# Four 64x64 tiles for the transitions of a delta-rule scan, and a recurrence split over two blocks

## The reference, cut to what matters

```python
def step(s, inp):
    r_t, w_t, k_t, v_t, kk_t, a_t = inp
    sa = jnp.einsum('bhvk,bhk->bhv', s, -kk_t)
    s = (s * w_t[:, :, None, :] + sa[..., None] * (kk_t * a_t)[:, :, None, :]
         + v_t[..., None] * k_t[:, :, None, :])
    return s, jnp.einsum('bhvk,bhk->bhv', s, r_t)
```

## Time and profile before

| what | us |
|---|---|
| median of three runs | 2008.89 |
| the profiled execution | 2013.03 |
| its span, first to last instruction | 2011.1 |
| transitions, first matmul to the last copy | 245.8 |
| one turn of the transitions | 29.3 |
| scan, to the first work of the attention | 35.6 |

### The profile page before, as it was taken

One profiled execution on the slowest core, in us unless ns is written; L12 is line 12 of the kernel. 1 busy time (PEld: TensorE's weight loads), 2 busy tenths in 40 slices (PEclk: granted clock), 3 DMA queues, 4 the chain that ended last, 5 costly groups with the idle time before them and its releaser, 6 DMA issues.

```text
span 2011.1 us, 45987 instructions
## 1 busy us (share of the span) xinstructions
PE 1839.5 (91%) x19492; PEld 1740.4 (87%) x19492; DVE 1058.7 (53%) x1790; ACT 812.6 (40%) x1442; POOL 280.9 (14%) x288
## 2 busy tenths in 40 slices
PE   5999999689999688884898999999999999999996
PEld 4988888589999467762898999999999999999995
DVE  4355554334554566657255776652247766432654
ACT  4233322122332266664244564542345555422442
POOL 0012121129990200001000000000000000000000
PEclk8999999899999698886898999999999999999997
DMA  4333434360002686644242343224335322333342
GB/s 152 101 124 121 147 110 141 130 198 4 4 4 49 167 232 185 197 129 173 95 157 72 129 132 133 88 86 137 123 109 173 133 85 94 104 111 106 122 149 87
DMA packets 100570, 241.03 MB, mean 120 GB/s; under 512 B 14290, under 2 KB 18770, under 8 KB 100082
## 3 DMA queue, kind: packets, MB, share of 16 engines
q1 hardware_dynamic: 99794, 235.96, 36.5%
q10 hardware_dynamic: 576, 2.16, 0.3%
HBM read 189.87 MB, written 48.21 MB: 118 GB/s over the span
## 4 chain that ended last, share of the span: by engine, by line
PE 48%; DVE 2%; ACT 1%; issue 1%; POOL 0%; ACTq 0%; DVEq 0%
PE tl_acc L2123 46%; PE tl_ple L2123 1%; PE tl_wide L2088 1%; PE tl_wide L2097 1%; ACT tl_wh L2272 0%; DVE tl_tmp L2396 0%; ACT tl_sq_e L2135 0%; DVE tl_gated L2458 0%; DVE tl_gated L2461 0%; DVE tl_Y L2378 0%; DVE tl_Y L2369 0%; ACT tl_Hh L2241 0%; DVE tl_acc_e L2302 0%; ACT tl_Y L2221 0%; ACT tl_sq_x L2135 0%
## 5 line engine op out<-in xcount | busy, mean ns | idle before, releaser
L2123 PE MATMUL tl_acc<-tl_Hh,tl_wh 128*128 128x264 f32 x1536 | 438.4, 285 | 7.4 <-DVE tl_Hl L2400 7.4
L2123 PE MATMUL tl_acc<-tl_Hh,tl_wl 128*128 128x264 f32 x1536 | 438.0, 285 | 0.0
L2123 PE MATMUL tl_acc<-tl_Hl,tl_wh 128*128 128x264 f32 x1536 | 435.9, 284 | 0.0
L2442 DVE TENSOR_TENSOR tl_wl<-tl_raw,tl_wh 128x1024 fp32r<-128x1024 f32 (+2 forms) x182 | 206.1, 1132 | 419.2 <-ACT tl_wh L2272 419.0
L2272 ACT ACTIVATE tl_wh<-tl_raw 128x1024 fp32r<-128x1024 f32 (+2 forms) x182 | 178.9, 983 | 493.9 <-PE tl_acc L2123 453.9
L2123 PEld LDWEIGHTS tl_acc<-tl_Hh,tl_wh 128*128 128x128 f32 x1536 | 290.0, 189 | 8.7 <-DVE tl_Hl L2400 8.3
L2123 PEld LDWEIGHTS tl_acc<-tl_Hl,tl_wh 128*128 128x128 f32 x1536 | 290.2, 189 | 0.0
L2123 PEld LDWEIGHTS tl_acc<-tl_Hh,tl_wl 128*128 128x128 f32 x1536 | 289.9, 189 | 0.0
L2123 PE MATMUL tl_acc<-tl_Gl,tl_wh 128*128 128x264 f32 x704 | 200.3, 285 | 0.0
L2123 PE MATMUL tl_acc<-tl_Gh,tl_wl 128*128 128x264 f32 x704 | 200.3, 284 | 0.0
L2123 PE MATMUL tl_acc<-tl_Gh,tl_wh 128*128 128x264 f32 x704 | 200.1, 284 | 0.0
(11 more groups left out here) (368 smaller groups left out, 4390.8 us busy)
## 6 DMA issues: line engine op xcount, KB each, us to landing
tl_raw<-dram_w_up SPq DMA_DIRECT2D x88, 512.0 KB, 3.5
as_kT<-dram_k_pool SPq DMA_DIRECT2D x64, 256.0 KB, 3.3
as_vp<-dram_v_pool SPq DMA_DIRECT2D x64, 256.0 KB, 3.2
tl_raw<-dram_w_down SPq DMA_DIRECT2D x32, 448.0 KB, 3.4
dram_projT<-fr_cur SPq DMA_DIRECT2D x26, 528.0 KB, 2.9
fr_raw<-dram_w_in SPq DMA_DIRECT2D x52, 256.0 KB, 3.6
tl_raw<-dram_w_pg SPq DMA_DIRECT2D x32, 320.0 KB, 3.2
ap_dup<-dram_projT SPq DMA_DIRECT2D x16, 512.0 KB, 8.4
```

The source lines that it names most:

```text
L2123: last = nc.tensor.matmul(out[:, n, 0:HP], w[:, u % 2, k, :], z, start=(begin and q == 0), stop=(end and q == 2))
L2442: tt(wl[:, u % 2, 0:kt], raw[:, u % 3, 0:kt], wh[:, u % 2, 0:kt].bitcast(F32), ALU.subtract).then_inc(S["residued"], 1)
```

## The change

1. A head of the pairs 2 and 3 now writes the other half of the partitions (`away`). Four heads (`quads`) stand on four different 64x64 tiles of the array, two of them on the diagonal and two off it. From level to level rows and outputs swap between `home` and `away`. PSUM is regrouped into `even` and `odd`, with pairs 0, 1 and pairs 2, 3 in different banks.
2. `zs` no longer has the identity added by VectorE. The transposed `zs` and the products of level 0 are instead summed in PSUM with a product with `eye`. `tx` and `ux` are two products of 64x64 in place of one of 64x128. The factor 0.5 moves from `ws` to `tn` and `xs`.
3. VectorE masks `m2`, `m4` of a chunk right behind `zs` and waits for `vn_kept` of ScalarE first.
4. SyncE loads the samples' operands right behind the first two chunks, then four chunks, then ten. The constants (four now) are loaded from ScalarE's queue.
5. GpSimd does three of the four steps of the sample recurrence here and the fourth in the scan block. The store of the samples' results moves to the scan block too, behind the last state, and the read of `ysd` behind it. The low parts move to VectorE (`low`, at chunks 6, 8, 10, 12).

```diff
-        heads = [(p, half(h)) for p in range(NPAIR) for h in range(2)]
+        heads = [(p, h) for n in range(2) for p in (n, n + 2) for h in range(2)]
+        quads = (heads[:4], heads[4:])
+        home = lambda p, h: half(h)
+        away = lambda p, h: half(1 - h if p >= 2 else h)
...
-            samples.load(sp, a["wkv"], o["sd"], vec_in, state_in)
-            sp.wait_ge(recurred, NT * RECUR_STEPS)
-            samples.store(sp, o, y_out, state_out)
...
-            samples.recur(pool, recurred)
+            samples.recur(pool, recurred, 0, NT - 1)
...
+            def product(q, cols, w, z, rows, cells, quad=heads, start=True, stop=True):
+                for p, h in quad:
+                    r = rows(p, h)
+                    last = nc.tensor.matmul(q[cells(p, h), p // 2, p % 2, cols], w(r, p), z(r, p), start=start, stop=stop)
+                return last
...
+                for lev in range(NLEV):
+                    rows, cells = (away, home) if lev % 2 == 0 else (home, away)
...
+                        if lev == 0:
+                            for quad in quads:
+                                product(q1[b], left, z, u, rows, cells, quad, stop=False)
+                                product(q1[b], left, one, u, rows, cells, quad, start=False)
...
-                    dve.wait_ge(S["adi0"], c + 1)
-                    tt(zs[:, b], zs[:, b], pairs(eye[:]), ALU.add).then_inc(S["adi"], 1)
...
+                    dve.wait_ge(S["vn_kept"], i * 2 + b + 1)
+                    tt(four(m2[:, b]), q1[b][..., left], pairs(below[:]), ALU.mult).then_inc(S["m2"], 1)
...
             sp.wait_ge(S["state"], NCH)
             sp.dma_start(state_out, states[:, NCH]).then_inc(S["state_out"], 16)
+            sp.wait_ge(S["recurred"], RECUR_STEPS)
+            samples.store(sp, o, S["y_out"], S["sample_out"])
+            sp.dma_start(yt[:], o["ysd"].rearrange("t h a v -> t (h a v)")).then_inc(S["sample_in"], 16)
...
-            for c in range(2):
-                pool.wait_ge(S["high"], c + 1)
-                nc.gpsimd.tensor_tensor(qs[DH:P, 0, c], dup[DH:P, 0, c], qs[DH:P, 0, c].bitcast(F32), ALU.subtract)\
...
+            samples.recur(pool, S["recurred"], NT - 1, NT)
...
+                if c in LOW_AT:
+                    low(LOW_AT.index(c))
```

More of the change, by code:

```diff
@@ L1251, in rwkv_transitions @@
     nc = kit.nc
-    names = ("const_in", "adi0", "adi", "m3", "p1", "p2", "m2", "m4", "turned", "bk_kept", "vn_kept", "zturn", "ut", "made",
-             "zk", "a2v", "a2v_kept", "w", "tx", "tn_kept", "xs", "pr", "phi_kept", "r_kept", "zy", "z_kept", "y_kept")
+    names = ("const_in", "m1", "m3", "p1", "p2", "m2", "m4", "bk_kept", "vn_kept", "zturn", "ut", "made", "zk", "a2v", "a2v_kept",
+             "w", "tx", "ux", "tn_kept", "xs", "pr", "phi_kept", "r_kept", "zy", "z_kept", "y_kept")
     S = {n: kit.sem("rt_" + n) for n in names}
-    first_in, rest_in = kit.sem("rt_first_in"), kit.sem("rt_rest_in")
-    vec_in, state_in, halved, recurred, y_out, state_out = (
-        kit.sem("rt_" + n) for n in ("vec_in", "state_in", "halved", "recurred", "y_out", "state_out"))
+    first_in, next_in, rest_in = (kit.sem(f"rt_{n}_in") for n in ("first", "next", "rest"))
+    vec_in, state_in, halved, recurred = (kit.sem("rt_" + n) for n in ("vec_in", "state_in", "halved", "recurred"))
     with ExitStack() as ctx:
@@ L1307, in turn @@
             def turn(i, first):
                 here = [ds((i * 2 + b) * C, C) for b in range(2)]
+                one = lambda r, p: eye[r, :]
                 for b in range(2):
                     c = i * 2 + b
[L1311 to L1317, removed]
+                    now = here[b]
+                    nr = lambda r, p: NR[r, p, :, now]
+                    if not first:
+                        pe.wait_ge(S["phi_kept"], c - 1)
+                        pe.wait_ge(S["r_kept"], c - 1)
+                    product(q0[b], whole, lambda r, p: BK[r, 0, p, now], nr, home, away)
+                    product(q2[b], left, lambda r, p: BK[r, 0, p, now], one, home, away)
+                    product(q2[b], right, lambda r, p: BK[r, 1, p, now], one, home, away).then_inc(S["p1"], 1)
+                    if not first:
+                        pe.wait_ge(S["z_kept"], c - 1)
+                        pe.wait_ge(S["y_kept"], c - 1)
+                    product(q1[b], whole, lambda r, p: BK[r, 1, p, now], nr, home, away)
+                    product(q3[b], left, lambda r, p: V[r, p, now], one, home, away)
+                    product(q3[b], right, lambda r, p: NR[r, p, 0, now], one, home, away).then_inc(S["p2"], 1)
@@ L1318, in turn @@
                 for b in range(2):
                     c = i * 2 + b
[L1320 to L1328, removed]
@@ L1329, in turn @@
-                    last.then_inc(S["turned"], 1)
+                    z = lambda r, p: zs[r, b, p, :]
+                    pe.wait_ge(S["m1"], c + 1)
+                    pe.wait_ge(S["m4"], c + 1)
+                    for quad in quads:
+                        product(q1[b], left, z, one, away, away, quad, stop=False)
+                        last = product(q1[b], left, one, one, away, away, quad, start=False)
+                    last.then_inc(S["zturn"], 1)
+                for lev in range(NLEV):
+                    rows, cells = (away, home) if lev % 2 == 0 else (home, away)
+                    for b in range(2):
+                        c, n = i * 2 + b, (i * NLEV + lev) * 2 + b
+                        z = lambda r, p: zs[r, b, p, :]
+                        u = lambda r, p: ut[r, b, p, :]
+                        pe.wait_ge(S["ut"], n + 1)
+                        if lev == 0:
+                            for quad in quads:
+                                product(q1[b], left, z, u, rows, cells, quad, stop=False)
+                                product(q1[b], left, one, u, rows, cells, quad, start=False)
+                            pe.wait_ge(S["bk_kept"], c + 1)
+                            for quad in quads:
+                                product(q0[b], left, u, z, rows, cells, quad, stop=False)
+                                last = product(q0[b], left, u, one, rows, cells, quad, start=False)
+                            last.then_inc(S["made"], 1)
+                            continue
+                        if lev == NLEV - 1:
+                            product(q1[b], left, lambda r, p: m2[r, b, p, :], lambda r, p: vna[r, b, p, 0, :], away, away)\
+                                .then_inc(S["a2v"], 1)
+                        pe.wait_ge(S["zk"], (i * (NLEV - 1) + lev - 1) * 2 + b + 1)
+                        if lev < NLEV - 1:
+                            product(q1[b], left, z, u, rows, cells)
+                        product(q0[b], left, u, z, rows, cells).then_inc(S["made"], 1)
@@ L1330, in turn @@
                 for b in range(2):
                     c = i * 2 + b
[L1332 to L1358, removed]
@@ L1362, in turn @@
[L1362 to L1367, removed]
+                    t = lambda r, p: tn[r, b, p, :]
+                    x = lambda r, p: xs[r, b, p, :]
+                    kept = lambda n: lambda r, p: bkm[r, b, p, n, :]
@@ L1368, in turn @@
+                    v = lambda r, p: vna[r, b, p, 0, :]
                     pe.wait_ge(S["tn_kept"], c + 1)
[L1369 to L1372, removed]
+                    product(q0[b], left, t, kept(0), away, home)
+                    product(q0[b], right, t, kept(2), away, home).then_inc(S["pr"], 1)
@@ L1373, in turn @@
                     pe.wait_ge(S["xs"], c + 1)
[L1374 to L1378, removed]
+                    for quad in quads:
+                        product(q1[b], left, kept(0), x, away, home, quad, stop=False)
+                        product(q1[b], left, kept(1), v, away, home, quad, start=False)
+                        product(q1[b], right, x, kept(2), away, home, quad, stop=False)
+                        last = product(q1[b], right, v, lambda r, p: m4[r, b, p, :], away, home, quad, start=False)
@@ L1436, in _, with copy @@
         def _(act):
-            def copy(out, in_, sem):
-                nc.scalar.activation(out, in_, ACT.Copy).then_inc(S[sem], 1)
+            def copy(out, in_, sem, scale=1.0):
+                nc.scalar.activation(out, in_, ACT.Copy, scale=scale).then_inc(S[sem], 1)
             def turn(i, first):
@@ L1547, in add, with low @@
                 nc.vector.tensor_tensor(y, py[c % 2][:, :, 0:C], y, ALU.add).then_inc(S["y_added"], 1)
+            def low(n):
+                q, c = n // 2, n % 2
+                dve.wait_ge(S["high"], n + 1)
+                high, out = (qs, kh)[q], (qs, kl)[q]
+                rows = (slice(DH, P), slice(0, P))[q]
+                nc.vector.tensor_tensor(out[rows, 0, c], dup[rows, q, c], high[rows, 0, c].bitcast(F32), ALU.subtract)\
+                    .then_inc(S["low"], 1)
             nc.vector.memset(states[:, 0], 0.0).then_inc(S["zeroed"], 1)
@@ L1566, in _ @@
```

(4 more changed lines are left out.)

119 lines of the change are left out of this document (54 added, 65 removed).

## The result

The changed kernel takes 2045.9 us (median of four runs, 2043.0 to 2048.3), the kernel before 2008.0 beside it: ratio 1.017, 95% interval 1.015 to 1.020. It is slower, by 1.7%; the forecast was 1967 us. The profiled execution spans 2044.8 us against 2011.1, so 33.7 us more; the medians differ by 37.9, because the profiled execution of before (2013.0) lay 5.0 above the median of its four runs and that of after (2046.6) only 0.7.

A forecast was written before the change was run, and what follows sets the result against it. The prediction took TensorE to bound the transitions and a chain to bound the scan. Transitions −77 and scan +35 gave −42 us, 2008.9 to 1967 us; own range 1950 to 1990, eight in ten 1942 to 2020.

The forecast's parts named there:

- Pace of a pass: Transitions: on four tiles TensorE takes a 64-column pass every 14.6 ns, bounded above by 29 ns.
- the sum of a turn: Transitions: opening groups, levels and closing products add up to 19.1 us per turn in place of 29.3, gaining 10.2 us.
- Turn 0: First turn of the transitions: still starved of instructions during the large loads, so given a gain of only 5 us.
- The round trip through VectorE: Levels 1 to 4 of a turn: TensorE waits for VectorE's mask, 1.25 us per round, TensorE idle 0.3 us per level.
- Scan: Scan block: grows by 35 us, from GpSimd holding up VectorE's chain and from the store queued behind it.
- the exclusion: Scan: VectorE's instructions with both inputs in SBUF wait until GpSimd's current one is over, +22 us.
- the store: End of the scan: state write, samples' store and read of ysd queue on SyncE behind the last state, +13 us.
- (a): Rival, transitions: passes not issued at 14.6 ns in a long run but at 27 ns, turns 27.7 us, 2028 us; chance 0.11.
- (c): Rival, transitions: four tiles help by halves, fetching or loads being shared, 20 ns per pass, turns 22.8 us, 1994 us; chance 0.12.
- (b): Rival, transitions: matmul starts never closer than about 25 ns; as mechanism 27.3 ns, turns 26.2 us, 2017 us; chance 0.09.
- The sum: Whole kernel: transitions −77 us and scan +35 us make −42 us, from 2008.9 to 1967 us.

The follow-up runs named there:

- x8_recur_all: The changed kernel with all four recurrence steps in the transitions, so GpSimd is idle in the scan: 2021.2 us, 1.005 of the kernel before.
- x4b_strip64: Ahead of the transitions, TensorE alone runs 2048 passes of 64 columns in straight code, then a loop of 64 passes 32 times: 28.2 against 17.1 ns per pass.
- x3_merge: The changed kernel with tx and ux as one product and the two products of pr as one, same columns, 64 passes fewer per turn: 2028.8 us.
- x10_half: As x6_best, but VectorE adds the identity only for a turn's first chunk, TensorE sums it for the second: 1987.4 us, 0.987 of the kernel before.
- x12_merge_scan: The changed kernel with scan and store as before, tx and ux merged, pr merged, identity still summed by TensorE: 1996.4 us, 0.991 of the kernel before.
- x6_best: The changed kernel with scan, store and low parts as before, tx and ux merged, pr merged, identity added by VectorE: 1984.3 us, 0.988 of the kernel before.
- x5_dve_eye: The changed kernel with VectorE adding the identity to zs again, 864 passes per turn in place of 960: 2035.2 us, 1.011 of the kernel before.
- x11_no_recur: As x6_best, but GpSimd's sample recurrence is left out whole: 1970.1 us, 0.977 of the kernel before.

## Why the prediction was wrong

- **Pace of a pass: right for the array, wrong for the turn.** "I take 14.6 ns" holds wherever there are instructions (128 passes in a row). The step that failed is the next one, the sum of a turn from such paces: 19.1 us, measured 28.6. That sum had 7.5 packets of code in 19.1 us, one every 2.5 us; the trace of before has none less than 3.38 us behind the other, and its turns asked for one every 4.5. The number of passes was counted (480 per chunk in place of 416) and costed only as array time. The term that it put at nothing in all turns but turn 0 is the supply of code: 7.5 packets of 3.75 us, 28.1 of the 28.6 us.
- **Why the rows misled.** The 64 passes in 1.96 us of the earlier trace rows and the 8 in 0.24 are shorter than a packet of 128 passes, so they could not show the supply. The earlier trace rows did show it, 310 passes in 13.7 us, and I named instructions as what was short there, but took it for an effect of the large loads alone. They only made it worse: there the packets were 5.5 to 7.2 us apart.
- **Turn 0**, forecast 5 us shorter, got 3.7 longer (43.3 between first masks, before 39.6). While the loads run, the packets come 7 to 8 us apart (409.6, 417.5, 424.4, 431.4), and the turn needs 7.5 where it needed 6.5. The granted clock was 0.66 over it, before 0.91; what that cost beside the supply isn't shown.
- **The round trip through VectorE** as the next bound (0.3 us of waiting per level) was never reached: VectorE's mask was waited for 21 times in the levels of six turns, at most 0.2 us at a time.
- **Scan: right**, in both terms (+22 for the exclusion, measured 21.4; +13 for the store, measured 12.6; 34.0 in all), and x8_recur_all shows each for itself. The count behind the first was right as well: 12 products or low parts in the first 44 us, and 10 products and 2 low parts came. The low parts did take turns: the one at 674.27 lasted 5.08 us in place of 1.2, and the chain's next sum stood behind it.
- **Rivals.** None was the mechanism. (a), that 14.6 ns don't hold in a long run, came nearest, in the sign and in the turn (27.7), but as a slower pace with TensorE busy throughout, not as bursts and pauses; at 2028 it was 18 us short. (c) named shared fetching, but as a pace of 20 ns. (b): the Trainium skill, "TensorE: Matmul & The Clock Gate", section "Wait — 56ns, not 53.3ns?", has start-to-start never below about 25 ns. The traces disagree, for passes on different tiles: 14.6 ns over 128 passes on four tiles, and in the loop of x4b_strip64 three of four starts come 7 ns behind the one before. The average of 28 to 30 ns that looks like such a floor is a burst and a gap.
- **The sum**: −77 + 35 became −1 + 34 in the profiled executions; 4 of the 38 us between the medians come from their lying 5.0 and 0.7 us above their medians.

## What to carry to other kernels

Count TensorE's instructions, not only its columns: in straight code two per pass, and here 256 of them arrived every 3.7 us on the average, so that straight code whose passes take less than some 29 ns on the average (3.73 / 128) waits for code. Then fewer and wider products pay (x3_merge, 15 to 17 us). A short loop ran without the gaps in x4b_strip64; no run put the transitions themselves in one. Moving VectorE's work into extra products costs their share of a packet, and that has to be weighed against the wait that it saves: for one chunk of two it came out level (x10_half), for both it lost 1.4 us per turn (x12_merge_scan against x6_best). An instruction of VectorE with both inputs in SBUF doesn't belong on a chain beside a busy GpSimd (20 us over 16 products and 4 low parts here).

## What the runs showed of the hardware

- Straight code for TensorE came as one packet of 16 KB at a time, 3.2 to 4.5 us apart in turns 1 to 6 of the change; the packet itself took 0.9 to 1.5 us of that. The rest was a time from its landing to the first pass of the burst (1.2 to 1.5 us in x4b_strip64) and one from there to the next packet (mostly 1.0 to 1.6 us). What happens in these two wasn't found.
- A loop of 128 instructions ran for over 50 us without a single packet; a longer one wasn't tried.
- Four 64x64 tiles ran side by side at 14.6 ns per pass of 64 columns at 2.4 GHz. Passes of one column ran at a granted clock of 0.50 for all of 112 us, at 26.6 ns each in the loop.
- A wait of TensorE for another engine added to the supply's time instead of hiding in it (x5_dve_eye, x6_best, x11_no_recur), and no packet started across the long waits (8.2 us without one in x5_dve_eye, 8.0 in x6_best).
